# A hybrid mixer layer on one Trainium2 core: the first 16 adaptive-norm tiles multiplied on TensorE in pairs, and the last down weights split ahead of the last tile

## Chip, core and metric

The kernel runs on one core of a Trainium2 chip, which has eight. The metric is the device time of one execution in microseconds; the median of several runs is given.

## What is computed

One layer of a streaming encoder over 1024 frames of width 1024, float32. Cut to what the change touches:

```python
mod = silu(c) @ w_ada + b_ada                      # 6 x 1024 values
shift1, scale1, gate1, shift2, scale2, gate2 = split(mod, 6)
h = rms_norm(x, norm1_g) * (1 + scale1) + shift1
p = h @ w_in                                       # feeds four token mixers
...                                                # RG-LRU, stick-breaking attention, gated DeltaNet, RWKV-7
x = x + gate1 * (mixed @ w_out)
h = rms_norm(x, norm2_g) * (1 + scale2) + shift2
x = x + gate2 * ((gelu(conv3(h @ w_gate)) * (h @ w_up)) @ w_down)
return rms_norm(x, final_g)
```

## The kernel before

All activations lie transposed: a tile is 128 channels (partitions) by 1024 frames, and x is eight such tiles, `fa[:, 0:8]`. `fa` has 20 tiles of 1024 float32 columns that serve many uses in turn. The order of every engine is written out by hand, and semaphores join the engines.

Dense products run as three matmuls of a rounded format each: hi x hi, lo x hi and hi x lo. So every weight unit (128 x 1024) that DMA brings to `w_raw` is split by POOL into `w_hi` and `w_lo` (`split`, L500, in eight pieces, L512 and L516), and each activation tile is split into `h_hi` (ACT) and `h_lo` (DVE). `w_raw`, `w_hi` and `w_lo` have two slots each. A split of unit u waits until its raw unit has landed and until PE is done with the unit that held the slot (`used`). SP brings unit u when unit u-2 is split.

**The start.** SP queues the broadcast `c`, the ones mask, eight x tiles with two w_in units between them, and 16 tiles of `w_ada` transposed (rows are output channels), which use eight slots; then the masks and units 2 and 3. ACT makes Silu of `c` and squares the x tiles; PE adds the squares over the channels, tile by tile, with a matrix of ones in fp32 (L580). ACT makes 1/rms from that (`rstd1`). DVE reduces each of the 16 adaptive tiles against Silu(c) to one column of `mod` (L1670), adds the bias (L1674), makes `a1 = (1 + scale) * norm1_g` (L1678), and normalizes the x tiles (L1689). ACT applies `a1` and the shift twice, to `h_hi` (L1227) and to a float32 copy (L1231), and DVE takes the difference as `h_lo` (L1685), which counts `h_done`. The first dense group (L620) follows the k-tiles of h as they come: for each k, 2 units x 2 halves x 3 products of 512 columns. From unit 2 on, PE takes one unit after another (`in_unit`, L593). POOL splits units 0 and 1 into `ra` early (L519); the split of unit 2 waits for `h_done` 5 and `ada_used` 16.

**The end.** The FFN has 22 tiles. The gate and up units of each are multiplied (`ffn_tile`, `gemm`, L590), ACT and DVE make the convolution, gelu and product, and the down units are applied in groups of four tiles. The last tile and the one before it remain after the loop: `fin_down` (L1161, products at L1166) multiplies their two k-tiles with the last two down units, by output tile m and half of the frames. DVE adds each result to x (`fin_add`, L2273), ACT squares it (L1658), POOL sums the squares of a half (L570), PE sums that over the channels (`fin_sum`, L1171), ACT makes 1/rms (`fin_root`), and DVE normalizes (`fin_norm`, L2280). SP stores each half tile when it is done.

```python
for m in range(KT):                                # second half of the frames
    pe.wait_ge(sem("fin_add"), m + 1)
    fin_down(m, 1, 0)
    fin_down(m, 1, 1).then_inc(sem("fin_full"), 1)
    if m == 2:
        fin_sum(0, fin_bank[KT - 1])
fin_sum(1, fin_bank[0])
```

## Time and profile before

| | us |
|---|---|
| median of 3 runs | 1957.86 |
| lowest and highest | 1953.75, 1958.17 |
| the profiled execution's own time | 1957.07 |
| its span, first to last instruction | 1955.1 |

The profile shows one execution: busy time by engine (PE matmul, PEld its weight loads, DVE, ACT, POOL), timelines of each engine with what ended the idle time before an instruction, and tables of stretches with the clock that TensorE was granted.
### The profile page before, as it was taken

What the parts mean: (1) busy time and instruction counts of PE and PEld (TensorE: products, weight loads), DVE (VectorE), ACT (ScalarE), POOL (GpSimd) and SP (SyncE); (2) the same over time, 40 slices, a digit from 0 to 9 for tenths busy, and PEclk for the clock granted to TensorE, in tenths of its full rate; (3) what the DMA queues carried; (4) which work ended last, traced back from release to release, by engine and by line L of the source; (5) the groups of instructions that cost most, each with busy time, mean ns of one, the idle gap of its engine ahead of it and who ended that gap; (6) DMA issues with size and microseconds to landing.
All of it is one profiled execution on the core that took longest, in us unless ns stands there. A gap on an engine that the chain in (4) does not pass through costs nothing.

```text
span 1955.1 us, 33384 instructions
## 1 busy us (share of the span) xinstructions
PE 1878.0 (96%) x14012; PEld 1501.0 (77%) x14012; DVE 945.7 (48%) x1467; ACT 473.2 (24%) x735; POOL 914.1 (47%) x1100
## 2 busy tenths in 40 slices
PE   3999999999999999999999998999999999999995
PEld 1778777767887887887887786888888888888884
DVE  5865478754546546546545825432232323322325
ACT  4342344452212213213214305210100101101003
POOL 2656556523323223223225473455565646555645
PEclk7999999999999999999999999999999999999998
DMA  8435211232122122122125620111111111111112
GB/s 332 171 115 183 87 60 68 79 126 80 56 76 77 53 80 77 48 85 77 45 98 216 215 70 28 33 54 44 54 43 54 43 54 43 54 43 54 43 43 86
DMA packets 69686, 163.48 MB, mean 84 GB/s; under 512 B 5952, under 2 KB 30528, under 8 KB 69568
## 3 DMA queue, kind: packets, MB, share of 16 engines
q1 hardware_dynamic: 62080, 142.88, 21.7%
q10 hardware_dynamic: 7488, 18.88, 2.6%
q8 instruction: 92, 1.51, 0.3%
q14 instruction: 26, 0.21, 0.0%
HBM read 133.16 MB, written 28.57 MB: 83 GB/s over the span
## 4 chain that ended last, share of the span: by engine, by line
PE 47%; POOL 21%; issue 19%; DVE 7%; ACT 2%; DMA 1%; SPq 1%; POOLq 0%; ACTq 0%; DVEq 0%
PE gbank L590 32%; POOL w_hi L512 11%; POOL w_lo L516 10%; PE mbank L908 3%; DMA fa<-in_w_ada 1%; DVE state L2089 1%; PE gbank L1055 1%; DVE fa L1839 1%; PE gbank L908 1%; PE mbank L664 1%; PE mbank L831 1%; PE gbank L685 1%; DVE fa L1762 1%; DVE fa L2154 1%; PE mbank L1069 1%
## 5 line engine op out<-in xcount | busy, mean ns | idle before, releaser
L512 POOL TENSOR_TENSOR w_hi<-w_raw,zero 128x256 fp32r<-128x256 f32 (+1 forms) x520 | 397.1, 794 | 960.5 <-PE gbank L590 799.4
L590 PE MATMUL gbank<-h_hi,w_hi 128*128 128x512 f32 x1680 | 671.5, 400 | 2.7 <-POOL w_lo L516 2.7
L590 PE MATMUL gbank<-h_lo,w_hi 128*128 128x512 f32 x1680 | 661.3, 394 | 0.0
L590 PE MATMUL gbank<-h_hi,w_lo 128*128 128x512 f32 x1680 | 660.9, 393 | 0.0
L516 POOL TENSOR_TENSOR w_lo<-w_raw,w_hi 128x256 fp32r<-128x256 f32 (+1 forms) x520 | 460.8, 916 | 10.2
L590 PEld LDWEIGHTS gbank<-h_hi,w_hi 128*128 128x128 f32 x1680 | 316.0, 188 | 82.0 <-issue 14.8
L590 PEld LDWEIGHTS gbank<-h_hi,w_lo 128*128 128x128 f32 x1680 | 315.8, 188 | 68.3 <-issue 1.5
L590 PEld LDWEIGHTS gbank<-h_lo,w_hi 128*128 128x128 f32 x1680 | 316.2, 188 | 67.1 <-issue 3.1
L1146 PE MATMUL mbank<-ra,w_hi 128*128 128x512 f32 x640 | 197.0, 389 | 0.0
L1146 PEld LDWEIGHTS mbank<-ra,w_hi 128*128 128x128 f32 x640 | 120.1, 188 | 24.9
L2248 DVE SCALAR_TENSOR_TENSOR fa<-mbank,mod,fa 128x1024 f32<-128x1024 f32 x40 | 51.3, 1284 | 169.2 <-PE mbank L1146 169.2
L1146 PE MATMUL mbank<-ra,w_lo 128*128 128x512 f32 x320 | 124.5, 389 | 0.0
L1627 ACT ACTIVATE ra<-fa 128x1024 fp32r<-128x1024 f32 x22 | 23.3, 1061 | 333.8 <-PE mbank L1146 242.5
L2230 DVE TENSOR_SCALAR fa<-fa,cwc 128x1024 f32<-128x1024 f32 x20 | 23.0, 1151 | 156.7 <-ACT fa L1621 156.7
L2239 DVE TENSOR_TENSOR fa<-fa,gbank 128x512 f32<-128x512 f32 x44 | 30.2, 688 | 112.5 <-PE gbank L590 85.9
L908 PE MATMUL mbank<-fa 64*64 64x32 f32 (+1 forms) x3072 | 80.5, 221 | 0.5 <-DVE fa L2010 0.5
L908 PEld LDWEIGHTS mbank<-fa 64*64 64x64 f32 x3072 | 75.0, 134 | 6.2 <-issue 3.2
L1496 ACT ACTIVATE fa<-gbank,par 128x512 f32<-128x512 f32 x32 | 22.0, 689 | 211.4 <-PE gbank L590 211.4
L1621 ACT ACTIVATE fa<-gbank 128x512 f32<-128x512 f32 x44 | 26.3, 599 | 179.0 <-PE gbank L590 176.7
L1146 PEld LDWEIGHTS mbank<-ra,w_lo 128*128 128x128 f32 x320 | 60.1, 188 | 12.5
L1701 DVE CUSTOM_DVE_ANT_0 fa<-fa 128x1024 f32<-128x1024 f32 x32 | 46.2, 1488 | 22.5 <-ACT fa L1273 14.6
L1839 DVE TENSOR_TENSOR_SCAN fa<-fa 128x1024 f32<-128x1024 f32 (+7 forms) x32 | 47.9, 1498 | 1.1
(341 smaller groups left out, 2167.2 us busy)
## 6 DMA issues: line engine op xcount, KB each, us to landing
w_raw<-in_w_tail SPq DMA_DIRECT2D x74, 512.0 KB, 3.5
fa<-in_w_ada SPq DMA_DIRECT2D x48, 512.0 KB, 6.8
w_raw<-in_w_in SPq DMA_DIRECT2D x26, 512.0 KB, 4.2
p_scr<-fa ACTq DMA_DIRECT2D x20, 512.0 KB, 2.7
w_raw<-in_w_mix SPq DMA_DIRECT2D x16, 640.0 KB, 4.0
fa<-in_xT SPq DMA_DIRECT2D x16, 512.0 KB, 7.9
w_raw<-in_w_gate SPq DMA_DIRECT2D x16, 512.0 KB, 4.0
sig_scr<-fa ACTq DMA_DIRECT2D x32, 256.0 KB, 2.1
```

What stands on the lines that cost most here:

```text
L512: last = pool.tensor_tensor(hi[:, c], raw[:, c], zero[:, 0:1].to_broadcast([P, w]), ALU.add)
L516: last = pool.tensor_tensor(lo[:, c], raw[:, c], hi[:, c].bitcast(F32), ALU.subtract)
L590: mm = pe.matmul(gb[bank], w, r, start=(q == 0), stop=(q == 3 * ks - 1))
L908: return pe.matmul(o_, lhs[src, hc], r_, start=True, stop=True)
L1146: mm = pe.matmul(mb[2 * (ml % 2) + hf], w, x_, start=(q == 0), stop=(q == 3 * ks - 1))
L1621: act.activation(G[s_][:, 2 + hf * HALF:2 + (hf + 1) * HALF], gb[2 * hf], ACT.Copy).then_inc(sem("gate_read"), 1)
L1627: act.activation(ra[:, j, :], fa[:, 13 + s_, :], ACT.Copy).then_inc(sem("act_hi"), 1)
L1701: dve.tensor_tensor_reduce(slot, slot, fa[:, 11 if t < ADA_EARLY else 3, :], 1.0, 0.0, ALU.mult, ALU.add, mod[:, t:t + 1]).then_inc(sem("a ...
L1839: dve.tensor_tensor_scan(keep[:, ::-1], keep[:, ::-1], keep[:, ::-1], 1.0, ALU.mult, ALU.min).then_inc(sem("sb_scan"), 1)
L2230: dve.tensor_scalar(C[s_], G[s_][:, 2:2 + S], cw[2], None, ALU.mult).then_inc(sem("conv_steps"), 1)
L2239: dve.tensor_tensor(fa[:, 13 + s_, c], C[s_][:, c], gb[2 * hf + 1], ALU.mult).then_inc(sem("up_read"), 1)
L2248: dve.scalar_tensor_tensor(fa[:, m, :], mbank[:, bank:bank + 2, :].rearrange("p b s -> p (b s)"), mod[:, 40 + m:41 + m], fa[:, m, :], ALU. ...
```

## The change

At the start, the 16 adaptive tiles come in a second layout (`w_ada1`, rows are input channels) and in pairs, shift tile k and scale tile k. PE multiplies each pair with Silu(c) as a column (`c_col`, 128 x 8) in `shift_and_scale`: 16 fp32 products of one column, accumulated over eight blocks for each of the two tiles. The pair of tile k+1 stands ahead of the dense products of tile k. DVE adds the bias to two values, makes one `a1`, applies it together with 1/rms, and makes the low part of the tile before, from the normalized tile and the shift. DVE sums the squares of x, and PE sums them over channels once. ACT writes `h_hi` once and makes the broadcast Silu(c) behind all of h. The broadcast `c` comes after the fourth pair.

At the end, the last two down units are split into `ra` (slots 2, 3 for hi and 6, 7 for lo) as soon as the last group's down products are done. `fin_sum(0)` and its root stand one tile later; the last square of the second half goes to PE directly as a second product instead of through POOL's sum; one normalization fewer stands between the last additions.

```diff
@@ -353,23 +355,27 @@
                     sp.wait_ge(sem("ada_used"), t - 3)
                 sp.dma_start(fa[:, ADA_SLOT[t], :], a["w_ada"][t]).then_inc(sem(f"ada_in{t % 4}"), 16)
...
-            sp.dma_start(fa[:, 11, :], a["c"].to_broadcast([P, D])).then_inc(sem("c_in"), 16)
-            sp.dma_start(msk[:, M["ones"], :], a["masks"][:, M["ones"] * P:(M["ones"] + 1) * P]).then_inc(sem("ones_in"), 16)
             for k in range(KT):
                 sp.dma_start(fa[:, k, :], a["xT"][k]).then_inc(sem(f"x_in{k}"), 16)
-                if k < 2:
-                    unit("w_in", k, k, k)
-            for t in range(16):
-                if t >= 8:
-                    sp.wait_ge(sem("ada_used"), t - 7)
-                sp.dma_start(fa[:, 12 + t % 8, :], a["w_ada"][t]).then_inc(sem(f"ada1_in{t % 8}"), 16)
-                if t == 3:
+                if k == 0:
+                    sp.dma_start(c_col[:], a["c_col"]).then_inc(sem("c_col_in"), 16)
+                    sp.dma_start(msk[:, M["ones"], :], a["masks"][:, M["ones"] * P:(M["ones"] + 1) * P]).then_inc(sem("ones_in"), 16)
+                if k == 3:
+                    unit("w_in", 0, 0, 0)
+                elif k == 6:
+                    unit("w_in", 1, 1, 1)
+            for n, t in enumerate(ADA_FIRST):
+                if n >= 8:
+                    sp.wait_ge(sem("ada_used"), n - 7)
+                sp.dma_start(fa[:, 12 + n % 8, :], a["w_ada1"][t]).then_inc(sem(f"ada1_in{n % 8}"), 16)
+                if n == 1:
                     sp.dma_start(par[:], a["par"]).then_inc(sem("par_in"), 16)
+                elif n == 7:
+                    sp.dma_start(fa[:, 11, :], a["c"].to_broadcast([P, D])).then_inc(sem("c_in"), 16)
+            for u in range(2, 4):
+                unit("w_in", u, u % 2, u)
             sp.dma_start(msk[:].rearrange("p m c -> p (m c)")[:, 0:M["ones"] * P], a["masks"][:, 0:M["ones"] * P]).then_inc(sem("msk_in"), 16)
             sp.dma_start(msk[:].rearrange("p m c -> p (m c)")[:, (M["ones"] + 1) * P:], a["masks"][:, (M["ones"] + 1) * P:]).then_inc(sem("msk_in"), 16)
-            for u in range(2, 4):
-                unit("w_in", u, u % 2, u)
-
...
-            with pool.Fori(0, (UNITS - U_FFN) // 2 - 2) as i:
+            with pool.Fori(0, (UNITS - U_FFN) // 2 - 3) as i:
                 for n in range(2):
                     split(i * 2 + (U_FFN + 4 + n), n, i * 16 + 16 * (U_FFN // 2 + 3),
                           used=(sem("half_done"), i * 4 + (2 * KT + 6 + 2 * n)))
 
-            for n in range(2 * (KT - 1)):
+            for n in range(2):
+                u = UNITS - 2 + n
+                split(u, n, 16 * (u // 2 + 1), used=(sem("half_done"), NG * 2 * UG + (2 * KT + 4)), to=(ra[:, 2 + n, :], ra[:, 6 + n, :]))
+
+            for n in range(2 * (KT - 1) - 1):
...
-            for k in range(KT):
-                pe.wait_ge(sem("sq"), k + 1)
-                for hf in range(2):
-                    last = pe.matmul(mb[hf], m_("ones"), fa[:, 8 + 2 * (k % 2), hf * HALF:(hf + 1) * HALF],
-                                     start=(k == 0), stop=(k == KT - 1))
-                last.then_inc(sem("sq_used"), 1)
+            pe.wait_ge(sem("x_sq"), KT - 1)
+            for hf in range(2):
+                last = pe.matmul(mb[hf], m_("ones"), fa[:, 9, hf * HALF:(hf + 1) * HALF], start=True, stop=True)
+            last.then_inc(sem("sq_used"), 1)
...
+            def shift_and_scale(k):
+
+                if k == 0:
+                    pe.wait_ge(sem("cond_col"), 1)
+                if k >= 2:
+                    pe.wait_ge(sem("mod1"), k - 1)
+                for n in range(2):
+                    slot = (2 * k + n) % 8
+                    pe.wait_ge(sem(f"ada1_in{slot}"), 16 * (k // 4 + 1))
+                    for d in range(KT):
+                        last = pe.matmul(mb[2 + k % 2][:, n:n + 1], fa[:, 12 + slot, d * P:(d + 1) * P], c_col[:, d:d + 1],
+                                         start=d == 0, stop=d == KT - 1)
+                    last.then_inc(sem("ada_used"), 1)
...
-            pe.wait_ge(sem("w_split"), 2)
+            shift_and_scale(0)
             for k in range(KT):
+                if k < KT - 1:
+                    shift_and_scale(k + 1)
+                if k == 0:
+                    pe.wait_ge(sem("w_split"), 2)
                 pe.wait_ge(sem("h_done"), k + 1)
...
-                    w = (w_lo if which == 2 else w_hi)[:, m // 4, (m % 4 * 2 + k) * P:(m % 4 * 2 + k + 1) * P]
+                    w = ra[:, (6 if which == 2 else 2) + m // 4, (m % 4 * 2 + k) * P:(m % 4 * 2 + k + 1) * P]
...
-                pe.wait_ge(sem("fin_acc"), (hf + 1) * (KT - 1))
-                pe.matmul(bank, m_("ones"), fa[:, ACC, hf * HALF:(hf + 1) * HALF], start=True,
-                          stop=True).then_inc(sem("sq_summed"), 1)
+                pe.wait_ge(sem("fin_acc"), KT - 1 if hf == 0 else 2 * (KT - 1) - 1)
+                mm = pe.matmul(bank, m_("ones"), fa[:, ACC, hf * HALF:(hf + 1) * HALF], start=True, stop=hf == 0)
+                if hf == 1:
+                    pe.wait_ge(sem("fin_sq"), 2 * KT)
+                    mm = pe.matmul(bank, m_("ones"), fin_sq_slot(2 * (KT - 1) - 1), start=False, stop=True)
+                mm.then_inc(sem("sq_summed"), 1)
...
-                if m == 2:
+                if m == 3:
                     pe.wait_ge(sem("fin_add"), KT)
                     fin_sum(0, fin_bank[KT - 1])
...
-                    act.wait_ge(sem("sq_used"), k - 1)
-                act.activation(fa[:, 8 + 2 * (k % 2), :], fa[:, k, :], ACT.Square).then_inc(sem("sq"), 1)
+                if k >= 3:
+                    act.wait_ge(sem("x_sq"), k - 2)
+                act.activation(fa[:, 8 + 2 * (k % 2) if k else 9, :], fa[:, k, :], ACT.Square).then_inc(sem("sq"), 1)
...
-                act.activation(h_hi[:, k, :], fa[:, k, :], ACT.Identity, bias=mod[:, k:k + 1],
-                               scale=a1[:, k:k + 1]).then_inc(sem("h_hi"), 1)
-                if k >= 4:
-                    act.wait_ge(sem("h_done"), k - 3)
-                act.activation(fa[:, 12 + k % 4, :], fa[:, k, :], ACT.Identity, bias=mod[:, k:k + 1],
-                               scale=a1[:, k:k + 1]).then_inc(sem("h_f32"), 1)
+                act.activation(h_hi[:, k, :], fa[:, k, :], ACT.Identity, bias=mod[:, k:k + 1]).then_inc(sem("h_hi"), 1)
+            act.wait_ge(sem("c_in"), 16)
+            act.activation(fa[:, 11, :], fa[:, 11, :], ACT.Silu).then_inc(sem("cond"), 1)
+            act.preload_act_table_set("natural_log_exp_and_others")
...
+            for k in range(1, KT):
+                dve.wait_ge(sem("sq"), k + 1)
+                if k >= 2:
+                    dve.wait_ge(sem("x_sq"), k - 1)
+                dve.tensor_tensor(fa[:, 9, :], fa[:, 9, :], fa[:, 8 + 2 * (k % 2), :], ALU.add).then_inc(sem("x_sq"), 1)
+
+            def h_lo_in(k):
+
+                dve.wait_ge(sem("h_hi"), k + 1)
+                dve.scalar_tensor_tensor(h_lo[:, k, :], fa[:, k, :], mod[:, k:k + 1], h_hi[:, k, :].bitcast(F32), ALU.add,
+                                         ALU.subtract).then_inc(sem("h_done"), 1)
+
+            for k in range(KT):
+                b0 = PAR["b_ada"].start + k
+                dve.wait_ge(sem("par_in"), 16)
+                dve.wait_ge(sem("ada_used"), 2 * k + 2)
+                dve.tensor_tensor(mod[:, k:k + KT + 1:KT], mb[2 + k % 2][:, 0:2], par[:, b0:b0 + KT + 1:KT], ALU.add).then_inc(sem("mod1"), 1)
+                dve.wait_ge(sem("mod1"), k + 1)
+                dve.scalar_tensor_tensor(a1[:, k:k + 1], mod[:, KT + k:KT + k + 1], 1.0, pc("n1", k), ALU.add, ALU.mult).then_inc(sem("a1"), 1)
+                dve.wait_ge(sem("a1"), k + 1)
+                dve.wait_ge(sem("rstd1"), 1)
+                dve.scalar_tensor_tensor(fa[:, k, :], fa[:, k, :], a1[:, k:k + 1], fa[:, 9, :], ALU.mult, ALU.mult).then_inc(sem("h_norm"), 1)
+                if k:
+                    h_lo_in(k - 1)
+            h_lo_in(KT - 1)
             dve.wait_ge(sem("cond"), 1)
...
-            for t in range(16):
-                dve.wait_ge(sem(f"ada1_in{t % 8}"), 16 * (t // 8 + 1))
-                dve.tensor_tensor_reduce(fa[:, 12 + t % 8, :], fa[:, 12 + t % 8, :], fa[:, 11, :], 1.0, 0.0, ALU.mult,
-                                         ALU.add, mod[:, t:t + 1]).then_inc(sem("ada_used"), 1)
-            dve.wait_ge(sem("ada_used"), 16)
-            dve.wait_ge(sem("par_in"), 16)
-            dve.tensor_tensor(mod[:, 0:16], mod[:, 0:16], par[:, PAR["b_ada"].start:PAR["b_ada"].start + 16],
-                              ALU.add).then_inc(sem("mod1"), 1)
...
-            def h_lo_in(k):
-
-                dve.wait_ge(sem("h_f32"), k + 1)
-                dve.wait_ge(sem("h_hi"), k + 1)
-                dve.tensor_tensor(h_lo[:, k, :], fa[:, 12 + k % 4, :], h_hi[:, k, :].bitcast(F32), ALU.subtract).then_inc(sem("h_done"), 1)
-
-            dve.wait_ge(sem("rstd1"), 1)
-            for k in range(KT):
-                dve.tensor_tensor(fa[:, k, :], fa[:, k, :], fa[:, 9, :], ALU.mult).then_inc(sem("h_norm"), 1)
-                if k >= 2:
-                    h_lo_in(k - 2)
-            for k in range(KT - 2, KT):
-                h_lo_in(k)
...
-                if m >= 4:
-                    fin_norm(m - 4, 0)
-            for k in range(KT - 4, KT):
+                if m >= 5:
+                    fin_norm(m - 5, 0)
+            for k in range(KT - 5, KT):
...
+    t["c_col"] = f(cols(x["c"]))
+    t["w_ada1"] = f(tiles(x["w_ada"][0][:, 0:2 * D]))
```

The order of PE's instructions at the start, before: the sums of squares and the first dense products of tile 0 (`ra` holds the split weights of units 0 and 1).

```order
L580 MATMUL mbank<-fa,msk 128x512 [waits sq]
L580 MATMUL mbank<-fa,msk 128x512
L620 MATMUL gbank<-h_hi,ra 128x512 [waits h_done,w_split]
L620 MATMUL gbank<-h_lo,ra 128x512
L620 MATMUL gbank<-h_hi,ra 128x512 x2
```

And now, the ones-sum, pairs 0 and 1 and the start of tile 0; then the end of tile 0, pair 2 and the start of tile 1.

```order
L589 MATMUL mbank<-fa,msk 128x512
L602 MATMUL mbank<-c_col,fa 128x1 [waits ada1_in0,cond_col]
L602 MATMUL mbank<-c_col,fa 128x1 x7
L602 MATMUL mbank<-c_col,fa 128x1 [waits ada1_in1]
L602 MATMUL mbank<-c_col,fa 128x1 x7
L602 MATMUL mbank<-c_col,fa 128x1 [waits ada1_in2]
L602 MATMUL mbank<-c_col,fa 128x1 x7
L602 MATMUL mbank<-c_col,fa 128x1 [waits ada1_in3]
L602 MATMUL mbank<-c_col,fa 128x1 x7
L646 MATMUL gbank<-h_hi,ra 128x512 [waits h_done,w_split]
```

```order
L646 MATMUL gbank<-h_hi,ra 128x512
L602 MATMUL mbank<-c_col,fa 128x1 [waits ada1_in4,mod1]
L602 MATMUL mbank<-c_col,fa 128x1 x7
L602 MATMUL mbank<-c_col,fa 128x1 [waits ada1_in5]
L602 MATMUL mbank<-c_col,fa 128x1 x7
L646 MATMUL gbank<-h_hi,ra 128x512 [waits h_done]
```

The 16 products of a pair now stand between the dense products of two tiles, and a wait for `h_done` behind them.

DVE at the same place, before and now.

```order
L1678 SCALAR_TENSOR_TENSOR a<-mod,par 128x8 [waits mod1]
L1689 TENSOR_TENSOR fa<-fa 128x1024 [waits rstd1,a1]
L1689 TENSOR_TENSOR fa<-fa 128x1024 x2
L1685 TENSOR_TENSOR h_lo<-fa,h_hi 128x1024 [waits h_hi,h_f32]
L1689 TENSOR_TENSOR fa<-fa 128x1024
```

```order
L1709 TENSOR_TENSOR mod<-mbank,par 128x2 [waits ada_used,par_in]
L1711 SCALAR_TENSOR_TENSOR a<-mod,par 128x1 [waits mod1]
L1714 SCALAR_TENSOR_TENSOR fa<-fa,a 128x1024 [waits rstd1,a1]
L1702 SCALAR_TENSOR_TENSOR h_lo<-fa,mod,h_hi 128x1024 [waits h_hi]
L1709 TENSOR_TENSOR mod<-mbank,par 128x2 [waits ada_used,par_in]
```

The low part of a tile now stands behind the `mod`, `a1` and normalization of the next one, which wait for `ada_used`, counted by PE's pairs.

## Rows read from the trace of the kernel before

**Rows 1.** The page, part 1: busy time of each engine.
```profile
PE 1878.0 (96%) x14012; PEld 1501.0 (77%) x14012; DVE 945.7 (48%) x1467; ACT 473.2 (24%) x735; POOL 914.1 (47%) x1100
```

**Rows 2.** Timeline, PE, 0 to 100 us: start us, us, instruction, count, idle before, releaser.
```profile
8.86 15.61 PE L580 MATMUL mbank<-fa,msk 128*128 128x512 f32 x32 [8.86 <-ACT fa L1214]
46.82 0.77 PE L620 MATMUL gbank<-h_hi,ra 128*128 128x512 f32 x1 [22.36 <-DVE h_lo L1685]
...
71.42 0.39 PE L590 MATMUL gbank<-h_hi,w_hi 128*128 128x512 f32 x1
```

**Rows 3.** Timeline, DVE, 0 to 100 us.
```profile
20.59 1.22 DVE L1670 CUSTOM_DVE_ANT_0 fa<-fa 128x1024 f32<-128x1024 f32 x1 [20.59 <-DMA fa<-in_w_ada]
...
40.04 1.22 DVE L1670 CUSTOM_DVE_ANT_0 fa<-fa 128x1024 f32<-128x1024 f32 x1
...
41.31 0.18 DVE L1674 TENSOR_TENSOR mod<-mod,par 128x16 f32<-128x16 f32 x1
...
41.72 3.50 DVE L1689 TENSOR_TENSOR fa<-fa 128x1024 f32<-128x1024 f32 x3
45.45 1.23 DVE L1685 TENSOR_TENSOR h_lo<-fa,h_hi 128x1024 fp32r<-128x1024 f32 x1 [0.23 <-ACT fa L1231]
```

**Rows 4.** Timeline, ACT, 0 to 100 us.
```profile
12.79 1.06 ACT L1214 ACTIVATE fa<-fa 128x1024 f32<-128x1024 f32 x1 [1.50 <-DMA fa<-in_xT]
14.07 1.06 ACT L1214 ACTIVATE fa<-fa 128x1024 f32<-128x1024 f32 x1 [0.22 <-DMA fa<-in_xT]
...
24.50 1.26 ACT L1220 ACTIVATE fa<-mbank,eps 128x512 f32<-128x512 f32 x2 [1.02 <-PE mbank L580]
25.80 1.06 ACT L1223 ACTIVATE fa<-fa 128x1024 f32<-128x1024 f32 x1
```

**Rows 5.** Timeline, PE weight loads, 0 to 50 us.
```profile
9.85 0.34 PEld L580 LDWEIGHTS mbank<-fa,msk 128*128 128x128 f32 x1 [0.52 <-issue]
10.70 0.34 PEld L580 LDWEIGHTS mbank<-fa,msk 128*128 128x128 f32 x1 [0.52 <-issue]
...
46.79 0.29 PEld L620 LDWEIGHTS gbank<-h_hi,ra 128*128 128x128 f32 x1 [23.16 <-issue]
46.96 0.33 PEld L620 LDWEIGHTS gbank<-h_lo,ra 128*128 128x128 f32 x1
```

**Rows 6.** Timeline, PE, 434.8 to 436.5 us.
```profile
435.17 0.41 PE L775 MATMUL mbank<-tk,msk 128*128 128x32 f32 x2
435.41 0.39 PE L776 MATMUL mbank<-tk,msk 128*128 128x32 f32 x2
```

**Rows 7.** Stretches: us, PE, PEld, DVE, ACT, POOL busy, PEclk, DMA share, GB/s.
```profile
46.80:52.60 5.80, 5.78 (x14) 4.54 (x15) 5.80 (x6) 5.80 (x6) 0.00 (x0) 0.50 0.00 0
52.60:71.40 18.80, 18.80 (x84) 15.54 (x83) 16.81 (x23) 10.74 (x13) 15.05 (x17) 1.00 0.38 125
1209.70:1213.10 3.40, 1.26 (x6) 1.00 (x6) 1.83 (x3) 3.34 (x6) 0.00 (x0) 1.00 0.00 0
1213.10:1216.50 3.40, 3.40 (x10) 2.62 (x9) 3.25 (x6) 3.30 (x6) 0.36 (x1) 0.51 0.00 0
```

**Rows 8.** Timeline, last 70 us: POOL, then PE, then DVE.
```profile
1887.93 2.83 POOL L516 TENSOR_TENSOR w_lo<-w_raw,w_hi 128x256 fp32r<-128x256 f32 x4
1895.42 3.76 POOL L512 TENSOR_TENSOR w_hi<-w_raw,zero 128x256 fp32r<-128x256 f32 x4 [4.67 <-PE gbank L590]
...
1906.30 2.32 POOL L512 TENSOR_TENSOR w_hi<-w_raw,zero 128x256 fp32r<-128x256 f32 x4 [3.35 <-PE gbank L590]
...
1942.18 1.39 POOL L570 TENSOR_TENSOR fa<-fa 128x512 f32<-128x512 f32 x1 [0.28 <-ACT fa L1658]
...
1912.37 1.22 PE L1166 MATMUL mbank<-ra,w_hi 128*128 128x512 f32 x2 [6.16 <-POOL w_lo L516]
...
1931.55 1.10 PE L1171 MATMUL gbank<-fa,msk 128*128 128x512 f32 x2 [2.10 <-POOL fa L570]
...
1919.36 2.73 DVE L2273 SCALAR_TENSOR_TENSOR fa<-mbank,mod,fa 128x512 f32<-128x512 f32 x4 [9.66 <-PE mbank L1166]
```

More of the change, by code:

```diff
@@ L57 @@
 ADA_EARLY = 35
+ADA_FIRST = [t for k in range(KT) for t in (k, KT + k)]
 ADA_SLOT = [(8, 16, 18, 19)[_t % 4] if _t < ADA_EARLY else 12 + _t % 4 for _t in range(48)]
@@ L196, in program @@
         a1 = sb("a1", [P, 16])
+        c_col = sb("c_col", [P, KT])
         sl = sb("sl", [P, 4])
@@ L1611, in _ @@
                                scale=a1[:, 8 + k:9 + k]).then_inc(sem("h_f32"), 1)
-                act.wait_ge(sem("h_f32"), KT + n + 1)
+                act.wait_ge(sem("h_f32"), n + 1)
                 act.activation(h_hi[:, k, c], fa[:, 12 + k % 4, c], ACT.Copy).then_inc(sem("h_hi"), 1)
@@ L1659, in _ @@
                                    fa[:, m, hf * HALF:(hf + 1) * HALF], ACT.Square).then_inc(sem("fin_sq"), 1)
-                    if hf == 1 and m == 2:
+                    if hf == 1 and m == 3:
                         fin_root(0, fin_bank[KT - 1])
@@ L1676, in _ @@
-            dve.wait_ge(sem("mod1"), 1)
-            dve.scalar_tensor_tensor(a1[:, 0:8], mod[:, 8:16], 1.0, par[:, PAR["n1"]], ALU.add, ALU.mult).then_inc(sem("a1"), 1)
-            dve.wait_ge(sem("a1"), 1)
-            def h_lo_in(k):
-                dve.wait_ge(sem("h_f32"), k + 1)
-                dve.wait_ge(sem("h_hi"), k + 1)
-                dve.tensor_tensor(h_lo[:, k, :], fa[:, 12 + k % 4, :], h_hi[:, k, :].bitcast(F32), ALU.subtract).then_inc(sem("h_done"), 1)
-            dve.wait_ge(sem("rstd1"), 1)
```

12 lines of the change are left out of this document (5 added, 7 removed).

## The prediction

> **What bounds the kernel now.** I read the page first: PE is busy for 1878.0 of 1955.1 us [rows 1]. An edit can only move the end where PE stands still or runs slowly, so I looked for such places in the timelines. Two lie where the change is.
>
> At the start PE makes its sums of squares from 8.86 us, stands for 22.36 us, and begins the first dense group at 46.82. That group is eight k-steps of 12 products for two weight units; it gives way to the next unit at 71.42, which I call the mark [rows 2]. DVE decides it: 16 reductions from 20.59 to 41.20, then 0.41 us for the two small operations of `mod` and `a1`, then normalization at 1.17 us a tile and the low part; the group starts 1.37 us after the first low part [rows 3].
>
> At the end PE stands for 6.16 us before the last down products, for POOL's last split, and restarts at half clock [rows 8].
>
> **Start: when pair 0 is there.** ACT's squares at 12.79 and 14.07 waited on DMA, so a tile of 512 KB lands every 1.28 us [rows 4]. The first adaptive tile landed at 20.59 as the twelfth such transfer. In the new order (eight x, two w_in, two adaptive) the twelfth completes pair 0, again about 20.6, and x tile 7 lands two earlier, at 18.0. A square (1.06) and one DVE addition (1.2) give the total at 20.4, with all earlier ones done as the tiles land. PE then needs four passes over 512 columns. At half clock one pass took 10.70 - 9.85 = 0.85 us [rows 5]: 3.4 us, done at 23.8. ACT's two Ln and the Exp take from 24.50 to 26.86 [rows 4], so `rstd` is there at 26.3 and limits nothing below.
>
> **What a pair costs PE.** It is 16 fp32 products with one moving column. The ones-sum shows that each is two passes with a weight load of their own (32 records for 16 products [rows 2]). No row has one moving column. The nearest has 32 with the same 128x128 fp32 weights: two passes from 435.17 to 435.41, 0.24 us at full clock, most of it the load [rows 6]. 32 such passes are 3.8 us. At half clock two loads stood 0.17 us apart (46.79, 46.96) [rows 5]; the cost is 5.4 us by that and 7.7 if the whole 0.24 doubles. I take 4.6, between the first two.
>
> **The wait that takes the old one's place.** In PE's order `shift_and_scale(k+1)` stands behind the products of tile k-1 and ahead of those of tile k. The products of tile k need the low part of tile k. DVE makes that one behind `mod`, `a1` and the normalization of tile k+1, and these wait for pair k+1. So nothing overlaps: dense products (g), then a pair (s), then DVE's chain (D), then the next dense products. D is about 0.1 to wake, 0.41, 1.17 and 1.37 [rows 3]: 3.1 us, with scalar_tensor_tensor at the price of the tensor_tensor seen. The DMA, at 2.6 us a pair, is never the bound then. It happens for k = 1 to 6; tile 7's low part waits for no pair and lies beside tile 6.
>
> **The clock.** Twelve dense products take 12 x 18.8/84 = 2.7 us at full and 12 x 5.8/14 = 5.0 us at half clock [rows 7]. In the chain PE stands 3.1 us in every round. Such gaps cost the clock here: from 1209.7 to 1213.1 PE was busy 1.26 of 3.4 us, and the next stretch was granted 0.51 [rows 7]. It came back after a dense stretch: the start's group got half until 52.6 and full from there. I expect it to fall and rise in each round and take g between both levels, 3.9.
>
> Pair 0 and pair 1 are then done at 23.8 + 2 x 4.6 = 33.0, the first dense product starts at 36.1, and the mark comes at 36.1 + 8 x 3.9 + 6 x (4.6 + 3.1) = 113.5: **42.1 us later** than 71.4. Full clock throughout gives 23.8 + 7.6 + 3.1 + 21.6 + 6 x 6.9 = 97.5 (+26.1); half clock throughout 128.7 (+57.3) at 5.4 us a pair, and 147 (+75.7) at 7.7.
>
> Here the Trainium skill has a rule that speaks for the change (TensorE: Matmul & The Clock Gate, "Step-by-step: what each phase is for"): PE can pull a weight load ahead of matmuls in flight, when it goes to the background weight buffer. By it s would shrink towards nothing and the mark would nearly hold; the rival "nearly free" below is that case. No row has loads with a one-column product to test it; in [rows 6] short products did not hide theirs.
>
> **Other edits at the start, at nothing.** ACT drops eight h_f32 writes and DVE's low part reads one tensor more; both lie in D or beside it. The Silu of the broadcast c, with a table load, moves behind the last h_hi; it delays DVE's softplus by some 3 us beside the last dense products. POOL's split of units 2 and 3 waits for all 16 tiles, now until after pair 7, 2 x 3.9 + 3.1 = 10.9 us ahead of the mark, where a split takes 6.1 to 7.5 us [rows 8]. I take 0, with 0 to 2 us as bounds. The moved DMAs of c, the masks and units 2, 3 have that long to land. Behind the mark the order is the old one, so PE carries the delay to the end.
>
> **The tail.** POOL finished the up unit at 1887.93 + 2.83 = 1890.76 and then waited twice for PE to leave w_hi; its splits ran from 1895.42 to 1902.95 (7.5 us) and from 1906.30 to PE's start (6.1) [rows 8]. The target is now in `ra`, free since the last down group, and the raw units land a few us after their slots come free, the later one by 1895. Two splits of 6.1 to 7.5 us end by 1906, as PE finishes the up products. The 6.16 us go, and so does the half clock behind them: the first fin_add came 6.99 us after PE's restart, for 21 products that at 0.224 each need 4.7 and 0.2 to drain. It moves from 1919.36 to 1911.1: 8.2 us. `fin_sum(0)`, one tile later, finds its sum nearly ready (it waited 2.10 us): 1.5. At the very end POOL's addition of 1.39 us leaves the chain, while PE gains two passes beside DVE's normalizations of the first half: 1.4 less 0 to 1.7. Sum: **11 us earlier**, bounds 8 and 13; what is late next is DVE's row of 13 normalizations with nothing between them, and the stores.
>
> **Sum.** The profiled execution took 1957.07 us, 2 more than its span: 1957.1 + 42.1 - 11 = 1988.2; the median shown is 0.8 above that execution, so **1989**.
>
> **Rivals.**
> - *The clock stays full* (the one-column passes keep it up): +26.1 - 11 gives 1973. For it: PE's rests are only 3.1 us, if the products of a pair count as work. Against: [rows 7], where 2.1 us of rest in 3.4 cost the clock.
> - *The clock stays at half*: 2004 at 5.4 us a pair, 2022 at 7.7. Against it: five us of dense products at half clock have brought the clock back here.
> - *The pair is nearly free* and the kernel gets **faster**: loads slide under the dense products, or a pass is far shorter with one column. With s = 0 `rstd` binds the start: dense at 30.5, mark at 30.5 + 21.6 + 6 x 3.1 = 70.7, time 1946. It decides from a pair of 2.0 us (0.06 a pass) down, where the start's loss equals the tail's gain. For it: PE stands for 3.1 us a round, in which nothing else queues. Against: the pair needs its own wait to end and stands on the path itself.
> - *The tail does not do what it says*: a split of the last two units comes no earlier, because their DMA or `half_done` binds. Then the 6.2 us stay; 1998. Against it: the raw slots come free with the two splits before, the later at 1890.76 [rows 8].
>
> **Chances.** Forecast (1977 to 2004) 0.68; full clock 0.10; half clock 0.06; nearly free 0.11; in between, where start and tail cancel, 0.05. A measurement here tells 0.3% (6 us) from nothing. Faster 0.11, same 0.05, slower 0.84. The range 1966 to 2005 holds the forecast, the full clock with a dearer tail gain, and part of the half-clock case.
>
> **What would show it.** Right: x_sq's last addition at about 20.4 and the ones-sum ending near 24; groups of 32 one-column passes lasting 3.8 to 5.4 us; between them and the next dense group DVE's `mod`, `a1`, norm and low part in that order with PE idle about 3 us, six times; granted clock between half and full; L646's last product near 113; POOL writing `ra` before 1906 plus the shift; PE's wait on POOL's w_lo gone there. Wrong: dense groups following each other within 4 us, the DMA ending PE's waits, or a pair under 2 us.

## The result and the profile after

| | before | after |
|---|---|---|
| median of the timed runs | 1956.57 us (1953.75 to 1958.17, 4 runs) | 1998.05 us (1997.32 to 1998.36, 4 runs) |
| span of the profiled execution | 1955.1 us | 1996.2 us |
| mean granted TensorE clock | 0.986 | 0.978 |
| first dense product | 46.82 | 42.42 |
| the mark (first product of unit 2) | 71.42 | 123.86 |
| first fin_add | 1919.36 | 1962.73 |

The changed kernel takes 1.0213 of the time of before, with an interval of 1.0195 to 1.0231: **slower by 41 us**. The forecast was 1989, and its range of 1966 to 2005 holds the time.

The start. First PE's timeline; it answers to [rows 2]. Columns: start, us, engine, line, operation, tiles, count, and in brackets the idle time before and what ended it. L589 is the ones-sum, L602 the pairs, L646 the first dense group, L612 the units from 2 on.

```profile
25.21 3.75 PE L589 MATMUL mbank<-fa,msk 128*128 128x512 f32 x4 [25.21 <-DVE fa L1697]
28.76 10.54 PE L602 MATMUL mbank<-c_col,fa 128*128 128x1 f32 x64
42.42 0.76 PE L646 MATMUL gbank<-h_hi,ra 128*128 128x512 f32 x1 [3.13 <-DVE h_lo L1702]
...
47.01 4.45 PE L602 MATMUL mbank<-c_col,fa 128*128 128x1 f32 x32
54.49 0.80 PE L646 MATMUL gbank<-h_hi,ra 128*128 128x512 f32 x1 [3.03 <-DVE h_lo L1702]
...
59.77 3.72 PE L602 MATMUL mbank<-c_col,fa 128*128 128x1 f32 x32
66.52 0.80 PE L646 MATMUL gbank<-h_hi,ra 128*128 128x512 f32 x1 [3.04 <-DVE h_lo L1702]
...
115.63 0.80 PE L646 MATMUL gbank<-h_hi,ra 128*128 128x512 f32 x1 [3.85 <-DVE h_lo L1702]
...
123.86 0.39 PE L612 MATMUL gbank<-h_hi,w_hi 128*128 128x512 f32 x1
```

The first dense product comes 4.4 us earlier than before, and the mark 52.4 us later. Between them stands the same round six times: dense products (42.42 to 47.01), a pair (to 51.46), a rest of 3.0 us that DVE's low part ends (54.49). PE's waits, added up from 25 to 124 us, are these seven rests:

```profile
PE gbank L646 <- DVE h_lo L1702: 22.1, 7, 3.8
```

What DVE does in such a rest (its timeline; it answers to [rows 3]):

```profile
51.56 0.16 DVE L1709 TENSOR_TENSOR mod<-mbank,par 128x2 f32<-128x2 f32 x1 [9.28 <-PE mbank L602]
51.76 0.16 DVE L1711 SCALAR_TENSOR_TENSOR a<-mod,par 128x1 f32<-128x1 f32 x1
51.95 1.28 DVE L1714 SCALAR_TENSOR_TENSOR fa<-fa,a 128x1024 f32<-128x1024 f32 x1
53.15 1.28 DVE L1702 SCALAR_TENSOR_TENSOR h_lo<-fa,mod,h_hi 128x1024 fp32r<-128x1024 f32 x1
```

DVE stood 9.28 us for the pair, then made `mod`, `a1` and the normalization of the *next* tile, and only then the low part that PE was waiting for. That is the chain that the prediction read out of the order of the code.

The clock, in the windows view (length, busy time and count of each engine, granted clock, DMA share, GB/s):

```profile
29.10:32.50 3.40, 3.40 (x32) 3.40 (x31) 0.00 (x0) 2.23 (x3) 0.00 (x0) 1.00 0.25 40
32.50:46.20 13.70, 10.57 (x42) 9.74 (x42) 4.40 (x7) 2.29 (x2) 0.00 (x0) 0.50 0.44 145
46.20:49.60 3.40, 3.40 (x28) 3.23 (x28) 0.00 (x0) 0.00 (x0) 0.00 (x0) 1.00 0.00 0
49.60:59.80 10.20, 7.17 (x23) 5.92 (x23) 2.80 (x4) 1.15 (x1) 0.00 (x0) 0.50 0.32 103
...
34.00:39.00 5.00, 5.00 (x25) 5.00 (x25) 0.34 (x1) 1.15 (x1) 0.00 (x0) 0.50 0.62 201
```

Full and half clock alternate; from 32.5 to 121.3 the clock was at half for 68.4 of 88.8 us, in seven stretches. The first two rows hold a surprise. From 29.1 to 32.5 PE ran nothing but the passes of a pair, busy for 3.40 of 3.40 us, and *then* the clock fell to 0.50. The last row prices a pass at half clock: 25 passes in 5.0 us, 0.20 each, against 3.40 / 32 = 0.106 at full.

DVE's additions of the squares, and POOL's splits of units 0 and 1 beside them (timelines, one instruction a row, some left out):

```profile
11.62 1.23 DVE L1697 TENSOR_TENSOR fa<-fa 128x1024 f32<-128x1024 f32 x1
14.12 1.56 DVE L1697 TENSOR_TENSOR fa<-fa 128x1024 f32<-128x1024 f32 x1 [1.27 <-ACT fa L1243]
15.78 3.18 DVE L1697 TENSOR_TENSOR fa<-fa 128x1024 f32<-128x1024 f32 x1
...
21.90 3.17 DVE L1697 TENSOR_TENSOR fa<-fa 128x1024 f32<-128x1024 f32 x1
...
11.87 2.72 POOL L529 TENSOR_TENSOR ra<-w_raw,zero 128x1024 fp32r<-128x1024 f32 x1 [9.79 <-DMA w_raw<-in_w_in]
14.67 3.20 POOL L531 TENSOR_TENSOR ra<-w_raw,ra 128x1024 fp32r<-128x1024 f32 x1
...
20.79 3.20 POOL L531 TENSOR_TENSOR ra<-w_raw,ra 128x1024 fp32r<-128x1024 f32 x1
```

The first three additions took 1.22 to 1.23 us each; the last four, beside POOL's splits, took 10.95 us together. So the sum of squares was ready at 25.07.

The tail (timelines of POOL, PE, DVE, POOL, ACT; they answer to [rows 8]):

```profile
1942.36 2.32 POOL L518 TENSOR_TENSOR ra<-w_raw,zero 128x256 fp32r<-128x256 f32 x4
...
1952.36 2.83 POOL L522 TENSOR_TENSOR ra<-w_raw,ra 128x256 fp32r<-128x256 f32 x4
...
1957.70 2.88 PE L1192 MATMUL mbank<-ra 128*128 128x512 f32 x12
...
1962.73 2.73 DVE L2298 SCALAR_TENSOR_TENSOR fa<-mbank,mod,fa 128x512 f32<-128x512 f32 x4 [1.79 <-PE mbank L1192]
...
1982.48 1.41 POOL L580 TENSOR_TENSOR fa<-fa 128x512 f32<-128x512 f32 x1 [0.27 <-ACT fa L1684]
...
1986.80 0.69 ACT L1674 ACTIVATE fa<-mbank,eps 128x512 f32<-128x512 f32 x1 [2.71 <-PE mbank L1200]
```

POOL's splits into `ra` end at 1955.2, 2.5 us before PE goes from the up products straight into the last down products at 1957.70, with no rest and at full clock. DVE's last addition of the loop's down products (`fa<-mbank,mod,fa`, 128x1024) begins at 1936.15 against 1884.49, which is 51.66 later; the span is 41.1 longer; so the tail gives back 10.6 us.

### The profile page after: what moved, and what is told of

The parts are those of the page before. It is cut to its first block, busy times and chain, and to the rows that moved or that the text cites. A ratio compares the mean times of both kernels' runs of the same rounds, so it can differ in the third digit from the quotient of the medians.

```text
span 1996.2 us, 33838 instructions
## 1 busy us (share of the span) xinstructions
PE 1911.6 (96%) x14242; PEld 1538.8 (77%) x14242; DVE 943.0 (47%) x1456; ACT 466.7 (23%) x730; POOL 919.3 (46%) x1099
## 4 chain that ended last, share of the span: by engine, by line
PE 84%; DVE 8%; issue 3%; POOL 2%; ACT 2%; DMA 1%; SPq 1%; POOLq 0%; ACTq 0%; DVEq 0%
PE gbank L612 55%; PE mbank L1172 11%; PE mbank L934 3%; PE mbank L602 2%; PE gbank L646 2%; DVE state L2114 1%; PE gbank L1081 1%; DVE fa L1864 1%; POOL w_hi L518 1%; POOL fa L580 1%; PE gbank L934 1%; PE mbank L690 1%; PE mbank L857 1%; PE gbank L711 1%; DVE fa L1787 1%
## 5 line engine op out<-in xcount | busy, mean ns | idle before, releaser
L612 PE MATMUL gbank<-h_hi,w_hi 128*128 128x512 f32 x1680 | 670.8, 399 | 3.3 <-POOL w_lo L522 3.3
L612 PE MATMUL gbank<-h_lo,w_hi 128*128 128x512 f32 x1680 | 660.7, 393 | 0.0
L612 PE MATMUL gbank<-h_hi,w_lo 128*128 128x512 f32 x1680 | 660.3, 393 | 0.0
L522 POOL TENSOR_TENSOR w_lo<-w_raw,w_hi 128x256 fp32r<-128x256 f32 (+1 forms) x512 | 455.2, 919 | 10.0
L612 PEld LDWEIGHTS gbank<-h_hi,w_hi 128*128 128x128 f32 x1680 | 315.6, 188 | 82.5 <-issue 14.8
L612 PEld LDWEIGHTS gbank<-h_hi,w_lo 128*128 128x128 f32 x1680 | 315.5, 188 | 68.4 <-issue 1.5
L612 PEld LDWEIGHTS gbank<-h_lo,w_hi 128*128 128x128 f32 x1680 | 315.8, 188 | 66.7 <-issue 3.1
L646 PE MATMUL gbank<-h_hi,ra 128*128 128x512 f32 x64 | 32.5, 582 | 22.1 <-DVE h_lo L1702 22.1
```

What stands on the lines that cost most here:

```text
L522: last = pool.tensor_tensor(lo[:, c], raw[:, c], hi[:, c].bitcast(F32), ALU.subtract)
L612: mm = pe.matmul(gb[bank], w, r, start=(q == 0), stop=(q == 3 * ks - 1))
L646: mm = pe.matmul(gb[2 * hf + s], ra[:, 2 * s + w, k * P:(k + 1) * P], r[:, k, hf * HALF:(hf + 1) * HALF], start=(k == 0 and w == 0 and r i ...
```

## The experiments

"Mark" is the start of the first product of unit 2, in the profiled execution. The kernel before was timed on the same chip beside every experiment, and ratios are to it. Marks of one and the same start differ by up to 2 us from one execution to the next: 71.42 before, 69.96 and 69.47 in E3 and E10, whose start is that of before.

### E1: the low part straight behind its own tile

```diff
                 dve.scalar_tensor_tensor(fa[:, k, :], ...).then_inc(sem("h_norm"), 1)
-                if k:
-                    h_lo_in(k - 1)
-            h_lo_in(KT - 1)
+                h_lo_in(k)
```

> The changed kernel with one thing moved on DVE: the low part of tile k is made right behind the normalization of tile k, no longer behind that of tile k+1. My theory (the six rounds are dense products, then a pair, then DVE's chain, because the low part waits for the next pair): PE no longer stands between a pair and the dense products, the six waits of 3.0 us go, and with them much of the half clock. First dense product at about 39.4 instead of 42.4, rounds of 6.3 (full clock) to 9 us instead of 12.2, mark (first product of unit 2) at 83 to 100 instead of 123.9, time 1960 to 1975 against 1998. Rival, pairs and clock and not the wait are the loss: only the waits go, 18 to 21 us, rounds of 9.2, time 1977 to 1980. Rival, another wait takes the place (ACT's h_hi now stands between normalization and low part): less than 5 us gained.

Measured 1974.18 us (1973.55 to 1975.88), ratio 1.0098 (1.008 to 1.0115); the mark at 100.22. PE's timeline and the windows:

```profile
38.74 0.77 PE L646 MATMUL gbank<-h_hi,ra 128*128 128x512 f32 x1
...
43.23 4.58 PE L602 MATMUL mbank<-c_col,fa 128*128 128x1 f32 x32
47.67 0.77 PE L646 MATMUL gbank<-h_hi,ra 128*128 128x512 f32 x1
```

```profile
28.60:32.00 3.40, 3.40 (x32) 3.40 (x32) 0.00 (x0) 2.29 (x3) 0.00 (x0) 1.00 0.22 59
32.00:42.30 10.30, 10.30 (x42) 9.54 (x43) 4.92 (x8) 2.30 (x2) 0.00 (x0) 0.50 0.55 185
```

No dense product waits any more, a round (from one tile's first dense product to the next one's) falls from 12.2 to 8.9 us on average, and 23.6 us of the 52.4 at the mark are gone. So the order of DVE's instructions made the rests: the wait that the prediction named, shown by taking it away. But the clock stays at half from 32.0 to 42.3, in which PE was busy for 10.30 of 10.30 us. So it was not the rests that made the clock fall. The mark came out just past the slow end of what was expected (100) and the time at it, since the rounds kept their half clock.

### E2: pairs two tiles ahead

```diff
             shift_and_scale(0)
+            shift_and_scale(1)
             for k in range(KT):
-                if k < KT - 1:
-                    shift_and_scale(k + 1)
+                if k < KT - 2:
+                    shift_and_scale(k + 2)
```

> The changed kernel with one thing moved on PE: the pair of tile k+2 stands ahead of the dense products of tile k instead of the pair of tile k+1; DVE's order is as in the change. My theory: it breaks the same circle from the other side. The low part of tile k waits for pair k+1, which is done a whole round earlier. The first dense product comes later by one pair (44 to 45 us), then PE runs without rests; mark at 84 to 101, time 1961 to 1976, within 4 us of the kernel that moves DVE's low part. If the waits were due to something else than the order (DVE too slow, the DMA), this run stays above 1990.

Measured 1977.21 us (1972.46 to 1979.63), ratio 1.0102 (1.0081 to 1.0124); first dense product 45.71, rounds of 8.9 us, mark 101.21, each just above what was expected; the time is 3 us above that of E1, with overlapping intervals. The same cure from PE's side: the chain is cut by either order. Three pairs ahead of the first dense product make that 3.3 us later than in the changed kernel and gain nothing that E1 has not.

### E3: the tail alone

The kernel before with the edits of the tail only (the last two units split into `ra`, their `used` count, the down products from `ra`, the last square added by PE).

> The kernel before with the edits at the tail alone (last two down units split into ra, fin_sum one tile later, last square past POOL's sum, one normalization fewer between). Theory: start as before, mark at 71.4; the tail is 10 to 11.5 us shorter as in the changed kernel's trace (first fin_add 8.3 us earlier): 1945 to 1947 against 1956.6. Rival, the tail's gain needs the later start or is partly an effect of it: under 8 us.

Measured **1944.89 us** (1943.48 to 1947.33), ratio 0.9949 (0.993 to 0.9968); mark 69.96 (71.4 expected). DVE's timeline:

```profile
1908.41 2.73 DVE L2280 SCALAR_TENSOR_TENSOR fa<-mbank,mod,fa 128x512 f32<-128x512 f32 x4 [1.79 <-PE mbank L1170]
```

The first fin_add comes after the same 1.79 us of wait as in the changed kernel. The two halves of the change are independent: the tail's gain is had without the start's loss.

### E4: PE's rest filled with work

```diff
+                if 1 <= k < KT - 1:
+                    pe.wait_ge(sem("ln1"), 2)
+                    for _ in range(8):
+                        pe.matmul(mb[0], ra[:, 0, 0:P], h_hi[:, 0, 0:HALF], start=True, stop=True)
                 pe.wait_ge(sem("h_done"), k + 1)
```

The eight products of 512 columns go to a bank that nobody reads; they add nothing to the result.

> The changed kernel with eight extra 512-column products between pair k+1 and the dense products of tile k, for k = 1 to 6, into a bank nobody reads; they add nothing to the result. They lie in PE's rest of 3.0 us and take 1.8 us at full, 3.4 at half clock. Theory A, the clock is lost by the rests: it stays full, rounds of 2.7 + 3.6 + 3.0 = 9.4 us, mark near 107, time near 1981, faster for doing more. Theory B, one-column passes count as rest for the clock (in the changed kernel's trace it fell after 3.4 us that held only such passes): the clock still falls in most rounds, g and s stay mixed and the rounds stay between 11.5 and 13 us; time 1994 to 2003.

Measured 1986.87 us (2 runs), ratio 1.016 (1.0137 to 1.0182), below the interval of the changed kernel; mark 115.37. These are 48 products more and 11 us less, between what the two theories had expected. PE's timeline (L645 are the extra products) and the windows:

```profile
50.36 3.82 PE L602 MATMUL mbank<-c_col,fa 128*128 128x1 f32 x32
54.04 3.65 PE L645 MATMUL mbank<-h_hi,ra 128*128 128x512 f32 x8
57.49 0.45 PE L650 MATMUL gbank<-h_hi,ra 128*128 128x512 f32 x1
```

```profile
50.80:54.20 3.40, 3.40 (x31) 3.40 (x32) 0.00 (x0) 0.00 (x0) 0.00 (x0) 1.00 0.25 60
54.20:57.60 3.40, 3.40 (x9) 2.58 (x10) 2.80 (x4) 1.15 (x1) 0.00 (x0) 0.50 0.68 239
57.60:64.40 6.80, 6.80 (x48) 6.18 (x47) 0.32 (x2) 0.00 (x0) 0.00 (x0) 1.00 0.16 57
```

Both theories were half right. The work in the gap brings the clock back in time for the dense products (full from 57.6), so a round takes 10.4 us on average instead of 12.2: the rests did not make the clock fall, but they put off its return. And the stretch right behind a pair is still at half clock, though PE does not rest there in the two rounds shown (in the later four it stands for 0.2 to 0.8 us behind the extra products). What both 50.80 to 54.20 here and 29.10 to 32.50 in the changed kernel have in common is that they hold only one-column passes. That speaks for theory B as the reason of the fall, and E6 puts it to the test.

### E5: E1 with the squares summed on PE, as before

```diff
-            pe.wait_ge(sem("x_sq"), KT - 1)
-            for hf in range(2):
-                last = pe.matmul(mb[hf], m_("ones"), fa[:, 9, hf * HALF:(hf + 1) * HALF], start=True, stop=True)
+            for k in range(KT):
+                pe.wait_ge(sem("sq"), k + 1)
+                for hf in range(2):
+                    last = pe.matmul(mb[hf], m_("ones"), fa[:, 8 + 2 * (k % 2), hf * HALF:(hf + 1) * HALF],
+                                     start=(k == 0), stop=(k == KT - 1))
```

and without DVE's additions (L1697).

> The kernel e1_low_own_tile, with the squares of x summed by PE tile by tile as in the kernel before, and no additions on DVE. It tests the 4.8 us by which the total of the squares came later than I had worked out (25.2 instead of 20.4). Theory: DVE's seven additions ran beside POOL's split of units 0 and 1 and took 2.7 us each instead of 1.2; without them POOL's pieces are as short as before (1.9 and 2.35 instead of 2.7 and 3.2) and 1/rms is ready some 5 us earlier, PE starts the pairs at 21 to 23 instead of 28.3. Mark at 91 to 96 instead of 100.2, time 1965 to 1970. Rival, the DMA's order (x tile 7 comes later than I think) sets it: less than 2 us gained.

Measured 1968.42 us (1966.61 to 1970.4), ratio 1.0057 (1.004 to 1.0074); mark 92.53, 7.7 us ahead of E1. POOL's timeline and PE's:

```profile
11.20 1.89 POOL L529 TENSOR_TENSOR ra<-w_raw,zero 128x1024 fp32r<-128x1024 f32 x1 [9.12 <-DMA w_raw<-in_w_in]
13.17 2.36 POOL L531 TENSOR_TENSOR ra<-w_raw,ra 128x1024 fp32r<-128x1024 f32 x1
```

```profile
21.31 9.29 PE L604 MATMUL mbank<-c_col,fa 128*128 128x1 f32 x64
```

Without DVE's additions the same splits take 1.89 and 2.36 us where they took 2.72 and 3.20, and the pairs begin at 21.31, right behind the sums, instead of at 28.32 in E1. Part of these 7.0 us is that E1 runs its ones-sum (24.78 to 28.32) behind the last addition, where E5 adds as the tiles come. The additions, then, had made POOL slow. That POOL made them slow is read from the rows of the changed kernel above and not from this run, which has no additions.

### E6: E1 with 64 moving columns a product

```diff
-                        last = pe.matmul(mb[2 + k % 2][:, n:n + 1], fa[...], c_col[:, d:d + 1],
+                        last = pe.matmul(mb[2 + k % 2][:, n * 64:(n + 1) * 64], fa[...],
+                                         c_col[:, d:d + 1].to_broadcast([P, 64]),
```

All 64 columns are the same; DVE reads one.

> The kernel e1_low_own_tile, with the column of Silu(c) repeated to 64 columns in every product of a pair (64 equal results, one is read). A pass then streams 64 times as much and loads the same weights. Theory A, products of one column count as rest for the clock: now the clock holds, a pair takes 3.5 to 3.7 us instead of 3.8 to 5.3, dense products of a tile 2.8 to 3.2 instead of 4.2 to 4.9; mark at 78 to 86 instead of 100.2, time 1952 to 1961. Theory B, the clock goes by the time PE has instructions or loads weights, and is lost by something else: nothing changes, 1972 to 1977. Theory C, a pass of 64 columns is longer by its columns: slower than 1977.

Measured 1959.41 us (1955.04 to 1960.35, 10 runs), ratio 1.001 (1.0 to 1.002); mark 82.39. PE's timeline and the windows:

```profile
28.03 7.25 PE L602 MATMUL mbank<-c_col,fa 128*128 128x64 f32 x64
...
42.45 0.48 PE L647 MATMUL gbank<-h_hi,ra 128*128 128x512 f32 x1
...
48.79 0.48 PE L647 MATMUL gbank<-h_hi,ra 128*128 128x512 f32 x1
```

```profile
27.70:34.50 6.80, 6.80 (x60) 6.56 (x59) 1.61 (x3) 3.29 (x4) 0.00 (x0) 1.00 0.49 161
34.50:43.50 9.00, 8.14 (x57) 7.36 (x56) 4.76 (x8) 1.33 (x2) 0.00 (x0) 1.00 0.58 181
```

One number changed, and the clock is full from 27.7 until behind the mark. 64 times the columns cost nothing: the 64 passes of two pairs take 7.25 us, where they took 10.54 with one column and a clock that fell on the way. A round falls from 8.9 to 6.3 us, the mark by 17.8 us, the time by 14.8 (17 by the ratios, since E1 was timed on another chip). So the one moving column was what the clock fell behind, as theory A of this run had it; theories B and C, no change or longer passes, are out.

### E7: E5 and E6 together

> The two before together: low part with its own tile, squares summed on PE, 64 columns a product. If both readings are right the effects add: pairs start near 22, rounds of 6.3 us, mark at 72 to 79, time 1946 to 1954, which takes back nearly all that the start of the change lost. If only one is right, it equals the better of the two within 3 us.

Measured 1953.02 us (1951.11 to 1954.9, 10 runs), ratio 0.9982 (0.9972 to 0.9991); mark 76.61, first dense product 30.33, rounds 6.3 us. The three causes found so far are gone, and the start is still 6.6 us behind that of E3: the first dense product comes 16.0 us earlier than there, but PE gives 3.5 us to each of six pairs between dense products, 21 us together. In E3 DVE makes them all ahead of the dense products, while PE stands.

### E8: pairs on DVE, h by k-tile

The kernel of E3, with DVE's 16 reductions in the order of the pairs (k, 8 + k), each pair followed by its `mod`, `a1` and normalization and the low part of the tile before; ACT writes `h_hi` alone.

> The kernel with the tail alone changed, whose start still reduces the adaptive tiles on DVE, but in pairs: two reductions, mod, a1, the normalization and the low part of the tile before, per k-tile; ACT writes h_hi once. It takes the change's idea, h by k-tile as pairs land, and leaves the products on DVE. DVE then has 8 x (2 x 1.29 + 0.4 + 2.4) = 43 us from 20.6 on, the low part of tile 7 at 64, mark at 67 to 70 instead of 71.4, time 1940 to 1944 against 1944.9. Rival: POOL's splits slow DVE's two-operand work or the first dense products run at half clock throughout because PE waits for each tile; mark 71 to 74, 1945 to 1948.

Measured 1948.61 us (1943.71 to 1949.83), ratio 0.9947 (0.993 to 0.9963); mark 72.99, where 67 to 70 was expected and 71 to 74 by the rival. 1/rms came late (DVE waited for it until 28.38) and a round on DVE took 5.27 us: PE waits for seven of eight tiles, 18.8 us in all. No gain over E3.

### E9 and E10: a pair split over two engines, beside E3 again

E9 is E7 with the scale tile of each pair reduced by DVE, between the normalization and the low part of a tile:

```diff
                 dve.scalar_tensor_tensor(fa[:, k, :], ...).then_inc(sem("h_norm"), 1)
+                if k < KT - 1:
+                    scale_tile(k + 1)
                 h_lo_in(k)
```

and PE multiplies the shift tile alone. The broadcast `c` and its Silu, which DVE's reduction needs, stand ahead of the squares again. E10 is the kernel of E3 once more.

> The version with the squares summed on PE, 64 columns a product and the tail of the change, but each pair split over two engines: PE multiplies the shift tile alone (8 passes pairs, 1.8 us), DVE reduces the scale tile (1.3 us) between the norm and the h_lo of a tile, where it covers ACT's h_hi. Theory (PE's own time in the pairs, 6 x 3.4 us behind the first dense group, is what was left between 76.6 and the kernel before): a round is PE's 2.7 + 1.8 = 4.5 us against 4.4 of DVE, first dense group near 30.5, mark near 30.5 + 7 x 4.5 + 2.7 = 64.7, time near 1940 us. Rival (DVE's longer chain sets the round, at 5.3 us or more, as with both reductions on DVE): mark at 70 or later, time 1945 to 1950, no better than the tail alone.

> The kernel before with the tail edits alone, once more, on the same chip as the run beside it: 1945 us again (first run 1944.89), 10 to 12 us under the kernel before. If the split of a pair over two engines is worth its 5 us, it comes out some 5 us below this one; if DVE bounds it, within 2 us or above.

Measured: E9 1944.54 us (1943.53 to 1945.49), ratio 0.9936 (0.992 to 0.9952); E10 1947.19 us (1943.62 to 1948.22), ratio 0.995 (0.9934 to 0.9966). The intervals overlap. E9's mark is at 69.49, as E10's 69.47. PE's timeline and a window of E9:

```profile
31.72 0.76 PE L648 MATMUL gbank<-h_hi,ra 128*128 128x512 f32 x1 [2.94 <-DVE h_lo L1698]
...
36.97 2.10 PE L604 MATMUL mbank<-c_col,fa 128*128 128x64 f32 x16
38.88 0.48 PE L648 MATMUL gbank<-h_hi,ra 128*128 128x512 f32 x1
...
43.44 0.48 PE L648 MATMUL gbank<-h_hi,ra 128*128 128x512 f32 x1
```

```profile
30.50:33.90 3.40, 2.18 (x5) 1.82 (x6) 3.36 (x5) 0.78 (x1) 0.00 (x0) 0.51 0.80 287
```

The round of 4.55 us came out as worked out (4.5). The mark did not (64.7 expected): the group starts 1.2 us later than assumed, its first tile runs at half clock (5.3 us instead of 2.7) behind a wait of 2.94 us, and the last tile waits 1.45 us for ACT's `h_hi`, since no reduction covers that one; together 5.2 us against 4.8 missed, with small terms of both signs beside them. E3 and E9 beat both kernels of this case, and the runs can't part them.

## Why the prediction was right, point by point

- **The wait that takes the old one's place: right.** D was put at 3.1 us, and PE's rests measured 3.03 to 3.13 in six of seven waits, with DVE's four operations in the order foretold. The seventh was 3.85, because POOL's split of unit 2, free to start since pair 7 was done, lay beside DVE's normalization (1.74 us instead of 1.28). E1 took the order away and the waits with it.
- **The start of the chain: 6.3 us too early, mis-sized.** The step was "a square (1.06) and one DVE addition (1.2) give the total at 20.4, with all earlier ones done as the tiles land". The total came at 25.07 and PE began its sum at 25.21, 4.8 us late. The addition's price of 1.2 held only for the additions that POOL's splits did not hold up. The ones-sum itself took 3.55 us (3.4 predicted), and pairs 0 and 1 added 1.3 (next point).
- **A pair: right in the mean.** 4.6 was taken; pairs 0 and 1 took 5.3 each (1.3 us more together) and the six in the rounds 3.7 to 4.7, mean 4.2 (2.4 less). The ends were 3.8 at full clock and 5.4 or 7.7 at half. A pass measured 0.106 us at full (3.4 a pair) and 0.20 at half (6.4): each pair was a mixture. A whole pair at half clock would thus be 6.4, between the two bounds of 5.4 and 7.7.
- **Dense products: g was 3.9, measured 4.84** (six rounds from 4.37 to 5.28; the last two tiles 8.23 together): 6.1 us more over eight tiles, and close to the 5.0 of half clock throughout: "between both levels" was the mis-sized term. With the waits' 0.4 the rounds took 6.1 - 2.4 + 0.4 = 4.1 us more than forecast, and 6.3 + 4.1 makes the mark 10.4 later than 113.5.
- **The clock: the direction right, its cause wrong.** "Such gaps cost the clock here" failed as the reason why it falls in each round. In E1 PE had no gaps and the clock was at half all the same; in E4 the gaps were filled and it fell behind the pairs all the same; in E6 the passes had 64 columns and it never fell. The rival "the clock stays full" had the right condition in its own words, "if the products of a pair count as work". With one column they did not keep it up. The fall is behind g's size too: the clock had come back only late in each tile's dense products, and the rest ahead of them put that off (E4). Rests can go ahead of a fall as well: in E9, with 64 columns, PE stood for 2.94 us ahead of 31.72, and the stretch from 30.5 to 33.9 was granted 0.51.
- **"Nearly free" is out.** The Trainium skill ("TensorE: Matmul & The Clock Gate", "Step-by-step: what each phase is for") has PE pull weight loads ahead of matmuls in flight. The trace shows what that leaves here: loads back to back for 3.40 of 3.40 us, at 0.106 each. 64 times the columns left that time as it was (E6), so it is the loads that are paid. The same page ("LDWEIGHTS (loading the stationary operand)") puts a load at its columns divided by 1.2, in ns; for 128 columns that is an estimate of 107 ns, and 3.4 us for the 32 loads of a pair. The trace agrees at full clock, and at half shows 0.20 us a load. The prediction drew on the first section and not on the second, which speaks against a free pair.
- **Edits put at nothing: 0 to 2 us allowed, some 0.8 us seen**, as the wait of 3.85 above. Behind the mark the kernel gave back 0.8 us (52.4 at the mark, 51.66 at DVE's last addition in the loop).
- **The tail: 11 predicted, 10.6 measured.** The first fin_add was put 8.2 us earlier; 1919.36 + 51.66 = 1971.02 against 1962.73 is 8.3. DVE's wait around `fin_sum(0)` fell from 3.81 to 2.50 (1.3, where 1.5 was put), and the way from the last fin_add to the final normalizations from 6.42 to 5.49 (0.9, where 1.4 less 0 to 1.7 was put). The rival "the tail does not do what it says" names 1998, the time measured, but that is chance: the split ended 2.5 us before PE needed it. Its sum is off as well; by the prediction's own terms 1957.1 + 42.1 - 11 + 8.2 + 0.8 is 1997, and with 6.2 instead of 8.2 it is 1995.
- **The total: 9 us above 1989, inside the range by 7.** The start was 10.4 us dearer than foretold and nothing made up for it; the time lies nearer to the rival "the clock stays at half" (2004) than to the forecast, and the clock was indeed at half for 68.4 of 88.8 us. The range held because it was drawn over that rival too, which is in part luck.

The sum: 1957.1 + 52.4 - 0.8 - 10.6 = 1998.1, the median measured. What the parts of the start are worth, each by the mark:

| kernel | mark | time | ratio to before |
|---|---|---|---|
| after | 123.86 | 1998.05 | 1.0213 |
| E1: + low part behind its own tile | 100.22 | 1974.18 | 1.0098 |
| E5: + squares summed on PE | 92.53 | 1968.42 | 1.0057 |
| E7: + 64 columns | 76.61 | 1953.02 | 0.9982 |
| E9: + scale tiles on DVE | 69.49 | 1944.54 | 0.9936 |
| E3: tail alone | 69.96 | 1944.89 | 0.9949 |

Of the start's 52.4 us DVE's order made 23.6, the sum on DVE 7.7, one-column passes 15.9, by this order of removal (64 columns were worth 17.8 behind E1 alone); the 5.2 us that are left to the 71.42 of before are PE's own time in the pairs, less the earlier first dense product. Not settled: only 1 and 64 columns were run, and why the first dense tile of E9 ran at half clock is read from one row and not tested.

## What to carry to other kernels

When a producer's work is cut into steps so that a consumer can start early, write down for each step what stands ahead of it on *both* queues: the consumer's next piece must not need something that is queued behind a wait for the consumer. Work moved to the engine that bounds the kernel is paid in full, even if it looks small there: in E7, with all else mended, six pairs of 3.5 us on PE cost 21 us and the earlier start gave 16. And keep the two halves of a change apart when you time it: this one held a gain of 11 us under a loss of 52.
